# A seventh weight place for the experts, over the residual and the routing scratch

## The chip, the cores and the metric

One core of one Trainium2 chip runs the whole program. The metric is device time in microseconds (us), the median of three runs. The core has TensorE (PE in the profile, its weight loads PEld), VectorE (DVE), ScalarE (ACT), GpSimd (POOL) and SyncE (SP); SyncE does nothing here but issue transfers. Sixteen DMA engines serve the queues of all of them: q1 is SyncE's, q10 is ScalarE's, q0 is GpSimd's.

## The reference

One layer of a hybrid decoder for 512 prompt tokens and 64 sample tokens of width 1024, all in float32. The change touches only its last part: the output projection with the residual, the mixture of experts, and the closing norm.

```python
def finish_layer(x, o_nsa, o_dn, g1, sh2, sc2, g2, lp):
    x = x + g1 * (jnp.concatenate([o_nsa, o_dn], axis=-1) @ lp['w_out'])
    return x + g2 * hier_moe(modulate(x, lp['norm_ffn_g'], sh2, sc2), lp)

def hier_moe(h, lp):
    ...
    for e in range(N_EXPERTS):
        he = jax.nn.silu(x @ lp['w_gate'][e]) * (x @ lp['w_up'][e])
        y = y + gates[:, e:e + 1] * (he @ lp['w_down'][e])
    return y.reshape(B, T, D)

y_prompt = rmsnorm(xp, final_norm_g)
```

The residual `x` after the projection is needed twice: at once, for the normalized rows that are routed, and at the very end, when the experts' sum is added to it. Each token picks one of 4 groups and 2 of its 8 experts. There are 32 experts with three matrices of 1 MiB each (gate, up, down), 1152 routed rows in all (2 for each of 576 tokens).

## The kernel before

The last stage (`stage_moe`, with a helper `slot_parts`) runs in four parts.

1. *Projection and residual*, tile by tile (4 tiles of 128 prompt tokens and one of 64 sample tokens). TensorE multiplies (L2416, L2420), VectorE adds the residual into `m.x2` (L2635), ScalarE squares and takes a root (L2577, L2579), VectorE normalizes into `h2` (L2646, L2647). ScalarE stores the normalized rows to DRAM (L2583, semaphore `h_out`).
2. *Routing.* VectorE and TensorE turn the logits into lists: which rows each expert works on, and which expert stands at which place (`permutation`, semaphore `perm_ok`). The index product is L2462, done with semaphore `ids_ps`. Most of its scratch lies in `m.aux`.
3. *The expert loop.* `ORDER` lists 49 places in a row: 32 base places (one expert each, up to 64 rows) and 17 attached ones, for the rows beyond 64 of an expert. An attached place shares its weights with the base place that `ATTACH` names and stands one base place behind it; if it has no rows, TensorE branches over its products and issues one small product (L2495, L2528) so that the order of the semaphores stays the same. For each place GpSimd gathers 64 rows from DRAM (L2386), TensorE turns them (L2470), multiplies with gate and up (L2483, L2484), turns the hidden rows (L2502) and multiplies with down (L2519, L2520); ScalarE applies silu (L2601) and copies the result out (`take_down`, L2593, L2594), GpSimd scatters it to DRAM (L2392).
4. *The closing.* SyncE loads the two chosen results of each token (L2349) into `rows`, TensorE mixes them with two diagonal matrices `diag` that hold the routing weights (L2561), VectorE scales and adds the residual (L2804 to L2810), then comes the final norm (L2816) and the store.

Weights go through a ring of `RING` places. With 6, they lie in three places of `m.ring`, in `m.late`, in `mod_r` (which holds the modulation rows first) and in `m.h2x` (the normalized rows first). The first `RING` experts are fixed and are loaded before the routing is known; the others are loaded by an index as soon as their place's earlier tenant has been multiplied (`follower`). SyncE issues all of it in the order of its program, each load behind the waits ahead of it. Experts 0 to 2 are asked for at the start, 3 when the projection is done (`y_ps`), 4 when the normalized rows are (`h_ok`), 5 when these have been turned and stored (`hT_ps`, `h_out`).

`m.x2` keeps the residual through the whole loop, and `m.aux` holds the ten diagonal tiles, which ScalarE makes in the middle of the loop (L2608). The closing uses `m.ring` place 2 as scratch (`end`) and reads the results into `m.ring` place 0 and `mod_r`.

Of the kernel before, what the change touches and what calls it, by code (L numbers as in the profile page):

```python
# [14 lines left out]
F32 = mybir.dt.float32  # L15
# [2138 lines left out]
TOPK = 2  # L2154
NOV = TOPK * NTOK // (T + 1)
NT = NE + NOV
RING = 6
KOV = -(-NTOK // T) - 1
DC = DE // P
SLOT = 2 * KD * DE + DC * D  # L2160
NDYN = NE - RING
NPAIR = 12
ATTACH = [RING + 2 * o for o in range(NPAIR)] + [RING + 3 + 4 * k for k in range(NOV - NPAIR)]
ORDER = [x for p in range(NE) for x in [("base", p)] + [("over", o) for o in range(NOV) if ATTACH[o] + 1 == p]]
PLACE = [x if kind == "base" else ATTACH[x] for kind, x in ORDER]
SLOT_OF = [p % RING for p in PLACE]
# [25 lines left out]
def stage_moe(nc, m, sb, sem, t, outs):  # L2192
# [6 lines left out]
    y_ps, x2_ok, sq_ok, rt_ok, h_ok, hT_ps, hT_ok, lg_ps = [sem("r_" + x) for x in ("y_ps", "x2_ok", "sq_ok", "rt_ok", "h_ok", "hT_ps", "hT_ok", "lg_ps")]  # L2199
    chain, pch, exp_in, exp_ok, cnt_ok, cnt_ps, rank_ps = [sem("r_" + x) for x in ("chain", "pch", "exp_in", "exp_ok", "cnt_ok", "cnt_ps", "rank_ps")]  # L2200
    lg_ok, ovf_ok, base_ps, put_ok, ids_ps, ids_ok, te_ok, choice_ok = [sem("r_" + x) for x in ("lg_ok", "ovf_ok", "base_ps", "put_ok", "ids_ps", "ids_ok", "te_ok", "choice_ok")]
    perm_ok = sem("r_perm_ok")
    gu_in, wd_in = [sem(f"gu_in{s}") for s in range(RING)], [sem(f"wd_in{s}") for s in range(RING)]
    r_in, y_out = [sem(f"e_r_in{i}") for i in range(XR)], [sem(f"e_y_out{i}") for i in range(YR)]
    t_ps, t_ok, gu_ps, silu_ok, he_ok, h_ps, heT_ok, dn_ps, yr_ok = [sem("e_" + x) for x in ("t_ps", "t_ok", "gu_ps", "silu_ok", "he_ok", "h_ps", "heT_ok", "dn_ps", "yr_ok")]
# [5 lines left out]
    with ExitStack() as ctx:  # L2211
# [16 lines left out]
        diag = m.aux[:, 0:TOPK * TILES * P].rearrange("p (c i n) -> p c i n", c=TOPK, n=P)  # L2228
        h2 = m.h2x[:, 0:TILES * D].rearrange("p (i n) -> p i n", n=D)
        ht = m.h2x[:, TILES * D:SLOT]  # L2230
        end = m.ring[:, 2]
        mod_f = end[:, 0:2 * D].rearrange("p (v k n) -> p v k n", v=2, k=1)
        fg, junk = end[:, 2 * D:3 * D], end[:, 5 * D:6 * D]
        moved = end[:, 3 * D:5 * D].rearrange("p (s n) -> p s n", s=2)
        rows = [a[:, 0:TILES * D].rearrange("p (i n) -> p i n", n=D) for a in (m.ring[:, 0], modr[:, :])]
        rwe, rwg = h2[:, PT, 0:KD * NE], h2[:, PT, KD * NE:KD * (NE + NG)]

        spare = m.mixT[:, :, :].rearrange("p c n -> p (c n)")
# [22 lines left out]
        same = bo2[0:1, 64:64 + NPAIR]  # L2261
# [13 lines left out]
        def _(sp):  # L2275
# [7 lines left out]

            def load_gate_up(n):
                kind, x = ORDER[n]
                wg, wu, wd = slot_parts(slots[SLOT_OF[n]])
                done = gu_in[SLOT_OF[n]]
                if kind == "base" and x < RING:
                    sp.dma_start(wg, t["expert_w_gate"][0, x].rearrange("(p k) n -> p k n", k=KD)).then_inc(done, 16)
                    sp.dma_start(wu, t["expert_w_up"][0, x].rearrange("(p k) n -> p k n", k=KD)).then_inc(done, 16)  # L2290
                else:
                    e, skip = expert(n)
                    sp.dma_start(wg, t["expert_w_gate"][0, bass.ds(e, 1)].rearrange("o (p k) n -> p (o k) n", k=KD), **skip).then_inc(done, 16)
                    sp.dma_start(wu, t["expert_w_up"][0, bass.ds(e, 1)].rearrange("o (p k) n -> p (o k) n", k=KD), **skip).then_inc(done, 16)

            def load_down(n):
                kind, x = ORDER[n]
                wg, wu, wd = slot_parts(slots[SLOT_OF[n]])
# [21 lines left out]
            load_base(3)  # L2320
            sp.wait_ge(h_ok, TILES)
            load_base(4)
            sp.wait_ge(hT_ps, TILES)
            sp.wait_ge(h_out, 16 * TILES)
            load_base(5)
            sp.wait_ge(perm_ok, 1)

            def follower(n):
# [12 lines left out]
            sp.wait_ge(dn_ps, LAST_USE[NE - RING] + 1)  # L2341
            spread_rows(sp, m, mod_f, 5, 1, f_in)
            sp.dma_start(fg, t["final_norm_g"].partition_broadcast(P)).then_inc(f_in, 16)
            for k in range(YR):
                sp.wait_ge(y_out[k], 16 * ((NT - k + YR - 1) // YR))
            for i in range(TILES):
# [57 lines left out]
        def _(pe):  # L2404
# [68 lines left out]
            def gate_up(n):  # L2473
                kind, x = ORDER[n]
                b = 2 + n % 2
                pe.wait_ge(t_ok, n + 1)
                if n >= 2:
                    pe.wait_ge(he_ok, n - 1)

                def products():  # L2480
                    for q in range(KD):
                        s = dict(start=(q == 0), stop=(q == KD - 1))
                        MM(PS[R, b, 0:DE], xT[:, n % 2, q, :], wg[:, q, :], **s)  # L2483
                        last = MM(PS[Q, b, 0:DE], xT[:, n % 2, q, :], wu[:, q, :], **s)  # L2484
                    return last

                wg, wu, wd = slot_parts(slots[SLOT_OF[n]])
# [17 lines left out]
            def down_products(n):  # L2505
# [4 lines left out]
                    pe.wait_ge(yr_ok, n - 1)  # L2510
                else:
                    pe.wait_ge(put_ok, 1)
                wd = slot_parts(slots[SLOT_OF[n]])[2]
                pe.wait_ge(wd_in[SLOT_OF[n]], 16 * LOADS[n])

                def products():
# [37 lines left out]
            for i in range(TILES):  # L2554
                r, b = ROWS[i], 2 * (i % 4)
                pe.wait_ge(row_in[i], 16 * TOPK)
                if i >= 4:
                    pe.wait_ge(a_ok, i - 3)
                for half in range(2):
                    for c in range(TOPK):  # L2560
                        last = MM(PS[0:r, b + half, :], diag[0:r, c, i, 0:r], rows[c][0:r, i, half * HALF:(half + 1) * HALF], start=(c == 0), stop=(c == 1))  # L2561
                    last.then_inc(f_ps, 1)

        @block.scalar
        def _(act):
# [4 lines left out]
            for i in range(TILES):  # L2570
                r = ROWS[i]
                if i == PT:
                    act.wait_ge(y_ps, TILES)
                    act.wait_ge(rw_ok, 1)
                    nc.scalar.copy(h2[R, PT, HALF:D], PS[Q, 2 * (PT % 2), :]).then_inc(split_ok, 1)
                act.wait_ge(x2_ok, i + 1)
                nc.scalar.activation(h2[0:r, i, :], m.x2[0:r, i, :], ACT.Square, accum_out=ssq[0:r, 0, i:i + 1]).then_inc(sq_ok, 1)  # L2577
                act.wait_ge(sq_ok, i + 1)
                nc.scalar.activation(ssq[0:r, 1, i:i + 1], ssq[0:r, 0, i:i + 1], ACT.Sqrt, scale=1.0 / D, bias=m.eps[0:r, 0:1]).then_inc(rt_ok, 1)  # L2579
            for i in range(TILES):  # L2580
                r = ROWS[i]
                act.wait_ge(h_ok, i + 1)
# [14 lines left out]
            for n in range(NT):  # L2597
# [3 lines left out]
                nc.scalar.activation(sg[Q, n % 2, :], PS[R, 2 + n % 2, 0:DE], ACT.Silu).then_inc(silu_ok, 1)  # L2601
                if n:
                    take_down(n - 1)
                if n == RING:
                    act.wait_ge(choice_ok, 1)
                    for c in range(TOPK):
                        for i in range(TILES):
                            last = nc.scalar.activation(diag[:, c, i, :], m.ident[:, :], ACT.Copy, scale=m.choice[:, c, i:i + 1])  # L2608
                    last.then_inc(diag_ok, 1)
            nc.scalar.activation(wgt[:, 0:1], m.eps[:, 2:3], ACT.Sqrt)  # L2610
            take_down(NT - 1)
            for i in range(TILES):
                r = ROWS[i]
                act.wait_ge(a_ok, i + 1)
# [5 lines left out]
        def _(dve):  # L2620
# [157 lines left out]
            def permutation():  # L2778
# [6 lines left out]
                link(V.tensor_tensor(same, pf[:, 0:2 * NPAIR:2], tef[:, 0:NPAIR], ALU.is_equal))  # L2785
                link(V.tensor_scalar(need, itf[:, :], be[0:1, 1, NE - 1:NE], None, ALU.is_lt))
                link(V.scalar_tensor_tensor(out=need[:, 0:NPAIR], in0=same, scalar=0.5, in1=need[:, 0:NPAIR], op0=ALU.is_lt, op1=ALU.mult))
                V.tensor_copy(pq[:, :], bo2[0:1, 0:NDYN + NOV]).then_inc(perm_ok, 1)

            take_x(0)  # L2790
# [8 lines left out]

            def add(i):  # L2800
                r, v, b = ROWS[i], VAR[i], 2 * (i % 4)
                if i == 0:
                    dve.wait_ge(f_ps, 1)
                    link(V.tensor_tensor(moved[0:r, 0, 0:HALF], PS[0:r, b, :], mod_f[0:r, v, 0, 0:HALF], ALU.mult))  # L2804
# [21 lines left out]
def build(nc, ins, outs):  # L2826
    t = ins
    with ExitStack() as ctx:
# [26 lines left out]
        m.seen = sb("seen", [P, 1])  # L2855
        m.gate_dram = nc.dram_tensor("gate_dram", [NB * TS, 24], F32)
        m.h2_dram = nc.dram_tensor("h2_dram", [NTOK + NT, D], F32)
        m.ys_dram = nc.dram_tensor("ys_dram", [LAST_ROW + 1, D], F32)
        m.choice = sb("choice", [P, TOPK, TILES])
        m.te = sb("te", [1, 2, NOV], I32)  # L2860
# [69 lines left out]
```

## Time and profile before

| | us |
|---|---|
| median of three runs (1067.5 to 1068.67) | 1068.22 |
| the profiled execution, its own time | 1060.37 |
| its span, first to last instruction | 1058.5 |
| TensorE busy in the span | 945.4 |
| VectorE, ScalarE, GpSimd busy | 449.0, 310.4, 268.7 |
| first and last product of the expert loop start | 757.19, 1018.57 |

Durations below come from the profiled execution. The page divides the span in 40 slices of 26.5 us; the expert loop lies in slices 29 to 39. Busy time is the union of an engine's instructions. A transfer has two times: when it is issued (a row of the issuing engine) and when it lands, which the profile tells through semaphores. A row of the chain of waits says who released the next step.

### The profile page before, as it was taken

What the parts mean: (1) busy time and instruction counts of PE and PEld (TensorE: products, weight loads), DVE (VectorE), ACT (ScalarE), POOL (GpSimd) and SP (SyncE); (2) the same over time, 40 slices, a digit from 0 to 9 for tenths busy, and PEclk for the clock granted to TensorE, in tenths of its full rate; (3) what the DMA queues carried; (4) which work ended last, traced back from release to release, by engine and by line L of the source; (5) the groups of instructions that cost most, each with busy time, mean ns of one, the idle gap of its engine ahead of it and who ended that gap; (6) DMA issues with size and microseconds to landing.
All of it is one profiled execution on the core that took longest, in us unless ns stands there. A gap on an engine that the chain in (4) does not pass through costs nothing. (4 is left out here: it accounts for less than half of the span.)

```text
span 1058.5 us, 21135 instructions
## 1 busy us (share of the span) xinstructions
PE 945.4 (89%) x8097; PEld 626.2 (59%) x8097; DVE 449.0 (42%) x933; ACT 310.4 (29%) x712; POOL 268.7 (25%) x397
## 2 busy tenths in 40 slices
PE   6899999998889899998799998996599989888955
PEld 5456777776656768986455664454355555445522
DVE  2330000013767257786478761446522233233317
ACT  4100000002674122333467541111023232333322
POOL 6000000132003048700356432000222333333310
PEclk9999999999999989999599998996599998899988
DMA  9977643433910030000744245908599999999854
GB/s 309 354 282 262 229 160 99 73 95 82 326 42 8 1 49 3 4 4 12 199 111 128 71 170 166 355 24 322 184 372 393 384 394 383 392 375 383 308 179 163
DMA packets 89225, 207.75 MB, mean 196 GB/s; under 512 B 31525, under 2 KB 54749, under 8 KB 75230
## 3 DMA queue, kind: packets, MB, share of 16 engines
q1 hardware_dynamic: 76226, 182.64, 49.4%
q0 software_dynamic: 10144, 20.47, 6.1%
q10 hardware_dynamic: 2756, 3.27, 0.9%
q8 instruction: 69, 1.13, 0.5%
q14 instruction: 30, 0.25, 0.1%
HBM read 254.83 MB, written 29.75 MB: 269 GB/s over the span
## 5 line engine op out<-in xcount | busy, mean ns | idle before, releaser
L2392 POOL DMA_INDIRECT ys_dram<-late,ids x49 | 45.3, 924 | 158.7 <-ACT late L2594 132.3
L592 PE MATMUL PS<-hT,wring 128*128 128x288 f32 x256 | 83.5, 408 | 0.0
L593 PE MATMUL PS<-hT,wring 128*128 128x288 f32 x256 | 83.0, 406 | 0.0
L2776 DVE COPY mixT<-PS 128x128 f32<-128x128 f32 x49 | 14.3, 291 | 155.7 <-PE PS L2502 99.3
L2386 POOL DMA_INDIRECT mixT<-h_dram,ids x49 | 46.9, 956 | 111.4 <-DVE ids L2743 92.4
L2483 PE MATMUL PS<-ring,mixT 128*64 128x256 f32 x304 | 71.4, 389 | 3.7 <-DVE mixT L2762 3.7
L2484 PE MATMUL PS<-ring,mixT 128*64 128x256 f32 x304 | 71.4, 389 | 0.0
L2483 PEld LDWEIGHTS PS<-ring,mixT 128*64 128x64 f32 x304 | 42.4, 141 | 34.1 <-issue 9.8
L2416 PE MATMUL PS<-late,mixT 128*128 128x512 f32 x128 | 58.4, 617 | 1.8 <-PEq L2843 1.8
L592 PEld LDWEIGHTS PS<-hT,wring 128*128 128x128 f32 x256 | 48.2, 190 | 17.2 <-DVE xc L203 2.6
L593 PEld LDWEIGHTS PS<-hT,wring 128*128 128x128 f32 x256 | 48.6, 190 | 13.4
L2593 ACT COPY late<-PS 64x512 f32<-64x512 f32 x49 | 28.3, 578 | 86.3 <-PE PS L2520 69.2
L629 POOL DMA_DIRECT2D late<-in_cache_cmp_k_dram x32 | 17.2, 538 | 132.0 <-issue 132.0
L2416 PEld LDWEIGHTS PS<-late,mixT 128*128 128x128 f32 x128 | 25.2, 199 | 33.0 <-issue 33.0
L2601 ACT ACTIVATE mixT<-PS 64x256 f32<-64x256 f32 x49 | 18.4, 376 | 89.2 <-PE PS L2484 55.9
L2762 DVE COPY mixT<-PS 128x512 f32<-128x512 f32 x49 | 33.8, 691 | 23.3 <-PE PS L2470 22.2
L2484 PEld LDWEIGHTS PS<-ring,mixT 128*64 128x64 f32 x304 | 42.4, 141 | 0.0
L201 DVE COPY xc<-PS 128x288 f32<-128x288 f32 x6 | 2.8, 458 | 92.1 <-PE PS L593 92.1
L2519 PE MATMUL PS<-ring,mixT 128*64 128x512 f32 x76 | 40.2, 655 | 1.0 <-DVE mixT L2776 0.8
L2470 PE MATMUL PS<-ident,mixT 64*128 64x64 f32 x392 | 35.6, 235 | 5.2 <-DMA mixT<-h_dram,ids 5.2
L2520 PE MATMUL PS<-ring,mixT 128*64 128x512 f32 x76 | 40.3, 656 | 0.0
L862 DVE SCALAR_TENSOR_TENSOR acc<-xc,convwT,acc 128x600 f32<-128x600 f32 x36 | 30.1, 843 | 11.6 <-ACT acc L781 10.5
(562 smaller groups left out, 2184.6 us busy)
## 6 DMA issues: line engine op xcount, KB each, us to landing
ring<-in_expert_w_gate_dram SPq DMA_DIRECT2D x27, 1024.0 KB
ring<-in_expert_w_up_dram SPq DMA_DIRECT2D x27, 1024.0 KB
ring<-in_expert_w_down_dram SPq DMA_DIRECT2D x27, 1024.0 KB
late<-in_w_ada_dram SPq DMA_DIRECT2D x8, 2048.0 KB
mod_r<-in_expert_w_gate_dram SPq DMA_DIRECT2D x9, 1024.0 KB
mod_r<-in_expert_w_up_dram SPq DMA_DIRECT2D x9, 1024.0 KB
mod_r<-in_expert_w_down_dram SPq DMA_DIRECT2D x9, 1024.0 KB
late<-in_expert_w_gate_dram SPq DMA_DIRECT2D x7, 1024.0 KB
```

The lines of the kernel that those rows point to most:

```text
L592: MM(PS[:, b, 0:HALF], lhs, hT[:, k, 0:HALF], **s)
L593: last = MM(PS[:, b + 1, 0:HALF], lhs, hT[:, k, HALF:NTOK], **s)
L862: ins = V.scalar_tensor_tensor(out=a, in0=m.xc[:, c, j:j + N], scalar=m.convwT[:, c, j:j + 1], in1=a, op0=ALU.mult, op1=ALU.add)
L2386: pool.indirect_dma_start(xr(n), None, m.h2_dram.ap(), bass.IndirectOffsetOnAxis(ap=ids[:, 0, j:j + 1], axis=0), bounds_check=NTOK + NT - ...
L2392: pool.indirect_dma_start(m.ys_dram.ap(), bass.IndirectOffsetOnAxis(ap=ids[:, 1, j:j + 1], axis=0), yr(n), None, bounds_check=LAST_ROW, oo ...
L2416: last = MM(PS[0:r, b + half, :], m.mixT[:, c, i * P:i * P + r], wo[:, c, half * HALF:(half + 1) * HALF], start=(c == 0), stop=(c == 7))
L2470: last = nc.tensor.transpose(PS[:, n % 2, c * T:(c + 1) * T], xr(n)[:, c * P:(c + 1) * P], m.ident[side(n), side(n)])
L2483: MM(PS[R, b, 0:DE], xT[:, n % 2, q, :], wg[:, q, :], **s)
L2484: last = MM(PS[Q, b, 0:DE], xT[:, n % 2, q, :], wu[:, q, :], **s)
L2519: MM(PS[R, b, :], heT[:, n % 2, c, :], wd[:, c, 0:HALF], **s)
L2520: last = MM(PS[Q, b, :], heT[:, n % 2, c, :], wd[:, c, HALF:], **s)
L2762: V.tensor_copy(xT[:, n % 2], PS[:, n % 2, :].rearrange("p (c n) -> p c n", n=T)).then_inc(t_ok, 1)
```

## The change

`RING` becomes 7. The seventh place lies over the first four tiles of `m.x2` (gate and up) and over `m.aux` (down). Expert 6 becomes a fixed one. ScalarE stores each prompt tile of the residual to DRAM (`x2_dram`) right after its root, and SyncE loads the four tiles back late in the loop; VectorE waits for each before it adds (`x_back`). The diagonal tiles move behind the last place of the loop and into `m.ring` places 0 and 1; the closing's scratch moves to `mod_r`. All attached places move back by one. `NPAIR` is only renamed.

```diff
-RING = 6
+RING = 7
...
+        diag = [m.ring[:, c, TILES * D:TILES * D + TILES * P].rearrange("p (i n) -> p i n", n=P) for c in range(TOPK)]
+        of_x2 = m.x2[:, :, :].rearrange("p i n -> p (i n)")
+
+        def parts(s):
+            if s < len(slots):
+                return slot_parts(slots[s])
+            return (of_x2[:, 0:KD * DE].rearrange("p (k n) -> p k n", n=DE), of_x2[:, KD * DE:2 * KD * DE].rearrange("p (k n) -> p k n", n=DE),
+                    m.aux[:, 0:DC * D].rearrange("p (c n) -> p c n", n=D))
...
-        end = m.ring[:, 2]
+        end = modr[:, :]
...
-        rows = [a[:, 0:TILES * D].rearrange("p (i n) -> p i n", n=D) for a in (m.ring[:, 0], modr[:, :])]
+        rows = [a[:, 0:TILES * D].rearrange("p (i n) -> p i n", n=D) for a in (m.ring[:, 0], m.ring[:, 1])]
...
             sp.wait_ge(h_ok, TILES)
             load_base(4)
+            sp.wait_ge(x_out, 16 * PT)
+            load_gate_up(6)
             sp.wait_ge(hT_ps, TILES)
             sp.wait_ge(h_out, 16 * TILES)
             load_base(5)
+            sp.wait_ge(ids_ps, 1)
+            load_down(6)
             sp.wait_ge(perm_ok, 1)
...
             sp.dma_start(fg, t["final_norm_g"].partition_broadcast(P)).then_inc(f_in, 16)
+            sp.wait_ge(dn_ps, LAST_USE[NE - RING + 2] + 1)
+            for i in range(PT):
+                sp.dma_start(m.x2[:, i, :], m.x2_dram.ap()[i * P:(i + 1) * P, :]).then_inc(x_back[i], 16)
...
                 nc.scalar.activation(ssq[0:r, 1, i:i + 1], ssq[0:r, 0, i:i + 1], ACT.Sqrt, scale=1.0 / D, bias=m.eps[0:r, 0:1]).then_inc(rt_ok, 1)
+                if i < PT:
+                    act.dma_start(m.x2_dram.ap()[i * P:(i + 1) * P, :], m.x2[:, i, :]).then_inc(x_out, 16)
...
-                if n == RING:
-                    act.wait_ge(choice_ok, 1)
-                    for c in range(TOPK):
-                        for i in range(TILES):
-                            last = nc.scalar.activation(diag[:, c, i, :], m.ident[:, :], ACT.Copy, scale=m.choice[:, c, i:i + 1])
-                    last.then_inc(diag_ok, 1)
             nc.scalar.activation(wgt[:, 0:1], m.eps[:, 2:3], ACT.Sqrt)
             take_down(NT - 1)
+            act.wait_ge(choice_ok, 1)
+            for i in range(TILES):
+                for c in range(TOPK):
+                    last = nc.scalar.activation(diag[c][:, i, :], m.ident[:, :], ACT.Copy, scale=m.choice[:, c, i:i + 1])
+            last.then_inc(diag_ok, 1)
...
             def add(i):
                 r, v, b = ROWS[i], VAR[i], 2 * (i % 4)
+                if i < PT:
+                    dve.wait_ge(x_back[i], 16)
```

How the instructions stand. First SyncE before the routing's result, from expert 4 (in `mod_r`) to the first read of the permutation (`pq`), before the change:

```order
L2289 DMA mod_r<-in_expert_w_gate_dram 128x2048
L2290 DMA mod_r<-in_expert_w_up_dram 128x2048
L2301 DMA mod_r<-in_expert_w_down_dram 128x2048
L2289 DMA h2x<-in_expert_w_gate_dram 128x2048
L2290 DMA h2x<-in_expert_w_up_dram 128x2048
L2301 DMA h2x<-in_expert_w_down_dram 128x2048
L2279 TENSOR_LOAD pq
```

And the same place after the change (`x` is `m.x2`, `h2x` holds expert 5):

```order
L2296 DMA mod_r<-in_expert_w_gate_dram 128x2048
L2297 DMA mod_r<-in_expert_w_up_dram 128x2048
L2308 DMA mod_r<-in_expert_w_down_dram 128x2048
L2296 DMA x<-in_expert_w_gate_dram 128x2048
L2297 DMA x<-in_expert_w_up_dram 128x2048
L2296 DMA h2x<-in_expert_w_gate_dram 128x2048
L2297 DMA h2x<-in_expert_w_up_dram 128x2048
L2308 DMA h2x<-in_expert_w_down_dram 128x2048
L2308 DMA aux<-in_expert_w_down_dram 128x2048
L2286 TENSOR_LOAD pq
```

Two transfers of 1 MiB have come in ahead of expert 5 and one behind it.

ScalarE at the end of the loop, from the load of the root's table to the closing's first square, before the change:

```order
L2610 ACT_TABLE_LOAD
L2610 ACTIVATE wgt<-eps 128x1
L2593 COPY late<-PS 64x512
L2594 COPY late<-PS 64x512
L2615 ACTIVATE ring,ssq_r<-x2 128x1024
```

And after it:

```order
L2620 ACT_TABLE_LOAD
L2620 ACTIVATE wgt<-eps 128x1
L2609 COPY late<-PS 64x512
L2610 COPY late<-PS 64x512
L2625 ACTIVATE ring<-ident,choice 128x128 x10
L2630 ACTIVATE mod_r,ssq_r<-x2 128x1024
```

The ten diagonal tiles now stand between the last copy of the loop and the closing. SyncE's last instructions after the change, from the modulation rows to the stores:

```order
L104 DMA mod_r<-mod_dram 128x1024
L106 DMA mod_r<-mod_dram 8x1024 x8
L2354 DMA mod_r<-in_final_norm_g_dram 128x1024
L2357 DMA x<-x_dram 128x1024 x4
L2363 DMA ring<-ys_dram 128x1024 x8
L2363 DMA ring<-ys_dram 64x1024 x2
L2367 DMA out_dram<-x 128x1024 x4
```

The line L2357 is new: the residual comes back between the norm's gain and the chosen results.

## Rows read from the trace of the kernel before

**Rows 1.** The page: busy tenths of the DMA engines in 40 equal slices.
```profile
DMA  9977643433910030000744245908599999999854
```

**Rows 2.** Stretches of the stage: us, busy time of each engine (instructions), clock, DMA share, GB/s.
```profile
core 0: us, PE busy (x) PEld busy (x) DVE busy (x) ACT busy (x) POOL busy (x), PEclk, DMA share, GB/s
690.00:718.00 28.00, 28.00 (x118) 14.33 (x116) 14.22 (x14) 2.89 (x6) 0.00 (x0) 1.00 0.02 7
742.00:752.00 10.00, 2.86 (x20) 2.42 (x20) 6.50 (x21) 0.00 (x0) 0.00 (x0) 0.50 0.79 315
752.00:754.00 2.00, 0.00 (x0) 0.00 (x0) 1.77 (x8) 0.00 (x0) 1.40 (x2) 0.50 0.00 0
764.00:980.00 216.00, 196.49 (x1590) 113.75 (x1592) 65.29 (x124) 65.80 (x133) 74.04 (x79) 0.95 1.01 381
1000.00:1005.00 5.00, 4.99 (x40) 2.54 (x40) 3.19 (x6) 1.91 (x4) 0.33 (x1) 1.00 0.42 166
```

**Rows 3.** Waits of TensorE in the expert loop: us in total, times, longest.
```profile
PE PS L2528 <- DVE mixT L2776: 9.7, 10, 1.7
PE PS L2483 <- DVE mixT L2762: 5.2, 8, 1.0
```

**Rows 4.** The chain of waits at the start of the loop: start us, us, what.
```profile
752.29 2.96 DMA mixT<-h_dram,ids
755.29 1.12 PE PS L2470 x8
757.19 0.69 PE PS L2483
```

**Rows 5.** Timeline of ScalarE, SyncE and TensorE: start us, us, engine line op.
```profile
712.40 0.29 ACT L2579 ACTIVATE ssq_r<-ssq_r,eps 128x1 f32<-128x1 f32 x1
...
726.85 0.50 SPq L2301 DMA_DIRECT2D mod_r<-in_expert_w_down_dram  x1
...
743.15 0.43 SPq L2301 DMA_DIRECT2D h2x<-in_expert_w_down_dram  x1
...
980.79 0.34 SPq L2293 DMA_DIRECT2D ring<-in_expert_w_gate_dram  x1
...
1004.25 0.34 SPq L104 DMA_DIRECT2D ring<-mod_dram  x1
...
1010.32 0.43 PE L2483 MATMUL PS<-ring,mixT 128*64 128x256 f32 x1 [0.36 <-DVE mixT L2762]
```

**Rows 6.** Queues from 728 to 742 us: packets, MB, share of the engines.
```profile
q1 hardware_dynamic: 481, 3.42, 59.1%
q10 hardware_dynamic: 603, 2.14, 37.4%
```

**Rows 7.** The five stores of the normalized rows (L2583).
```profile
DMA to landing us min/median/max: 8.6/15.1/17.8
```

**Rows 8.** The seventh gather; queues at 764.6 to 768, 768 to 770, 770 to 773.8.
```profile
764.68 0.94 POOL L2386 DMA_INDIRECT mixT<-h_dram,ids  x1 [4.73 <-PE PS L2470]
...
q1 hardware_dynamic: 107, 0.88, 71.3%
...
q0 software_dynamic: 26, 0.11, 15.4%
...
q0 software_dynamic: 54, 0.16, 16.0%
```

**Rows 9.** The ten diagonal tiles (L2608), and the chain of waits behind the loop.
```profile
L2608 ACT ACTIVATE aux<-ident,choice x10: 387/388/400, 802.4 to 805.0; 128x128 f32<-128x128 f32 x10
...
1019.91 0.59 ACT late L2594
1021.29 2.54 DMA ys_dram<-late,ids
...
1024.23 4.26 DMA mod_r<-ys_dram
1028.63 8.67 PE PS L2561 x16
```

More of the change, by code:

```diff
@@ L2161 @@
 NDYN = NE - RING
-NPAIR = 12
-ATTACH = [RING + 2 * o for o in range(NPAIR)] + [RING + 3 + 4 * k for k in range(NOV - NPAIR)]
+NMATCH = 12
+ATTACH = [RING + 2 * o for o in range(NMATCH)] + [RING + 3 + 4 * k for k in range(NOV - NMATCH)]
 ORDER = [x for p in range(NE) for x in [("base", p)] + [("over", o) for o in range(NOV) if ATTACH[o] + 1 == p]]
@@ L2201, in stage_moe @@
     lg_ok, ovf_ok, base_ps, put_ok, ids_ps, ids_ok, te_ok, choice_ok = [sem("r_" + x) for x in ("lg_ok", "ovf_ok", "base_ps", "put_ok", "ids_ps", "ids_ok", "te_ok", "choice_ok")]
-    perm_ok = sem("r_perm_ok")
+    perm_ok, x_out, x_back = sem("r_perm_ok"), sem("r_x_out"), [sem(f"f_x_back{i}") for i in range(PT)]
     gu_in, wd_in = [sem(f"gu_in{s}") for s in range(RING)], [sem(f"wd_in{s}") for s in range(RING)]
@@ L2227, in stage_moe @@
         bo2 = tmp_late[0:NE, 15 * D // 8:2 * D]
-        diag = m.aux[:, 0:TOPK * TILES * P].rearrange("p (c i n) -> p c i n", c=TOPK, n=P)
+        diag = [m.ring[:, c, TILES * D:TILES * D + TILES * P].rearrange("p (i n) -> p i n", n=P) for c in range(TOPK)]
[5 more added lines that the diff above has]
+                    m.aux[:, 0:DC * D].rearrange("p (c n) -> p c n", n=D))
         h2 = m.h2x[:, 0:TILES * D].rearrange("p (i n) -> p i n", n=D)
         ht = m.h2x[:, TILES * D:SLOT]
-        end = m.ring[:, 2]
+        end = modr[:, :]
         mod_f = end[:, 0:2 * D].rearrange("p (v k n) -> p v k n", v=2, k=1)
@@ L2260, in stage_moe @@
         pf, need = bo2[0:1, 0:NDYN], bo2[0:1, NDYN:NDYN + NOV]
-        same = bo2[0:1, 64:64 + NPAIR]
+        same = bo2[0:1, 64:64 + NMATCH]
         a4 = tb("a4", [P, TILES, NG])
@@ L2285, in load_gate_up @@
                 kind, x = ORDER[n]
-                wg, wu, wd = slot_parts(slots[SLOT_OF[n]])
+                wg, wu, wd = parts(SLOT_OF[n])
                 done = gu_in[SLOT_OF[n]]
@@ L2297, in load_down @@
                 kind, x = ORDER[n]
-                wg, wu, wd = slot_parts(slots[SLOT_OF[n]])
+                wg, wu, wd = parts(SLOT_OF[n])
                 done = wd_in[SLOT_OF[n]]
@@ L2485, in products @@
                     return last
-                wg, wu, wd = slot_parts(slots[SLOT_OF[n]])
+                wg, wu, wd = parts(SLOT_OF[n])
                 pe.wait_ge(gu_in[SLOT_OF[n]], 32 * LOADS[n])
@@ L2512, in down_products @@
                     pe.wait_ge(put_ok, 1)
-                wd = slot_parts(slots[SLOT_OF[n]])[2]
+                wd = parts(SLOT_OF[n])[2]
                 pe.wait_ge(wd_in[SLOT_OF[n]], 16 * LOADS[n])
@@ L2560, in _ @@
                     for c in range(TOPK):
-                        last = MM(PS[0:r, b + half, :], diag[0:r, c, i, 0:r], rows[c][0:r, i, half * HALF:(half + 1) * HALF], start=(c == 0), stop=(c == 1))
+                        last = MM(PS[0:r, b + half, :], diag[c][0:r, i, 0:r], rows[c][0:r, i, half * HALF:(half + 1) * HALF], start=(c == 0), stop=(c == 1))
                     last.then_inc(f_ps, 1)
@@ L2784, in permutation @@
                 link(V.tensor_scalar(pf, pf, -1.0, float(NE), ALU.mult, ALU.add))
-                link(V.tensor_tensor(same, pf[:, 0:2 * NPAIR:2], tef[:, 0:NPAIR], ALU.is_equal))
+                link(V.tensor_tensor(same, pf[:, 0:2 * NMATCH:2], tef[:, 0:NMATCH], ALU.is_equal))
                 link(V.tensor_scalar(need, itf[:, :], be[0:1, 1, NE - 1:NE], None, ALU.is_lt))
-                link(V.scalar_tensor_tensor(out=need[:, 0:NPAIR], in0=same, scalar=0.5, in1=need[:, 0:NPAIR], op0=ALU.is_lt, op1=ALU.mult))
+                link(V.scalar_tensor_tensor(out=need[:, 0:NMATCH], in0=same, scalar=0.5, in1=need[:, 0:NMATCH], op0=ALU.is_lt, op1=ALU.mult))
                 V.tensor_copy(pq[:, :], bo2[0:1, 0:NDYN + NOV]).then_inc(perm_ok, 1)
@@ L2857, in build @@
         m.h2_dram = nc.dram_tensor("h2_dram", [NTOK + NT, D], F32)
+        m.x2_dram = nc.dram_tensor("x2_dram", [SEQ, D], F32)
         m.ys_dram = nc.dram_tensor("ys_dram", [LAST_ROW + 1, D], F32)
```

## The prediction

> **What bounds the kernel now.** I read the page first. The DMA engines are full in the first quarter, nearly idle in the middle, and at nine tenths from slice 28 to slice 37, which is where the experts are worked through [rows 1]. That invites the reading "the expert loop waits for weights, so one more place for weights must help". The table by stretches sharpens it: from 764 to 980 us the DMA share is 1.01 at 381 GB/s, and TensorE is busy 196.5 of the same 216 us [rows 2]. Both are near their limit, so busy shares cannot say which of them sets the pace. The list of TensorE's waits in the loop can: its two largest entries are waits for a VectorE copy (9.7 and 5.2 us in total) [rows 3], and no weight tile stands anywhere in it. The larger is at L2528, the small product that an attached expert without rows still issues. So TensorE never meets a late weight; it loses time to the short dependent steps of the empty places and to its clock: a mean of 0.95 over 216 us [rows 2] is some 21.6 us at the lower level (0.05 x 216 x 2), which costs about 10.8 us.
>
> How far is the weight stream from being felt? The gate half of the last expert is asked for at 980.79 and first multiplied at 1010.32, after 0.36 us of waiting for a copy [rows 5]; the DMA share has fallen to 0.42 in 1000 to 1005 [rows 2]. So I take it that the last weights were there about 5 us before their use. That is the slack, and it is small: 5 of 243 us.
>
> At the front of the loop the chain of waits holds exactly one transfer. The indices are ready, the first gather is issued at 752.29, and 2.96 us later TensorE starts to turn its rows [rows 4]. From 752 to 754 the DMA engines move nothing, share 0.00 [rows 2]: the gather finds empty queues.
>
> **The change part by part.**
>
> *The seventh place.* It lets expert 6 (3.15 MB in gate, up and down) be loaded before the loop, so the loop streams 25 experts in place of 26. At 381 GB/s that is 3.15 / 0.381 = 8.3 us less streaming. But the list of waits shows nothing that ends when weights land, so by this profile it buys 0: it only raises the slack of 5 us.
>
> *Where its load lies.* Expert 6's gate and up are issued behind expert 4's, whose last part is issued at 726.85 [rows 5], and its down behind expert 5's, once the index product is done. In the kernel before, expert 5 is asked for at 743.15 (its last part) [rows 5] and those 3.15 MB move in 742 to 752 (0.315 x 10) [rows 2]; then the queue is dry. Now the same queue, served in order, has 2.1 MB ahead of expert 5 and 1.05 MB behind it: 3.15 MB more. The rate from 728 to 742 was (3.42 + 2.14) / 14 = 0.397 MB per us [rows 6], so the extra takes 7.9 us, of which about 2 us fill the gap between expert 5's issue and its first byte (8 us of transfer at that rate in a 10 us stretch). The queue is dry at about 752 + 7.9 - 2 = 758, not at 752. The first gather is still issued at 752.3, since nothing in the index chain changes, and now meets a full queue.
>
> What does a gather take beside full queues? The first one took 2.96 us. The seventh is issued at 764.68, just behind 2.1 MB of weights. Until 768 only the weight queue moves data (0.88 MB, no row of q0); the gather's queue moves 0.11 MB in 768 to 770 and 0.16 MB in 770 to 773.8 [rows 8]. It was not let through at its turn; it came in 5 to 9 us. The five 512 KB stores of the normalized rows, beside experts 3 and 4, took 8.6 to 17.8 us each [rows 7]. So I take it that the first gather lands when the weights ahead of it are through: at about 758.2 in place of 755.25, **+3.0 us**, straight on the path. Bounds: at the low end the gather gets a fair share. Then its at most 0.26 MB move at half of 0.397 MB per us in place of all of it: 1.3 us against 0.7, **+0.7**. At the high end it takes what the seventh took, up to 9.1 us: **+6.1**.
>
> The Trainium skill, "DMA: Bandwidth & Descriptors", section "Queues, rings and completion order", says that each DMA engine goes round between the queues that have work, a packet at a time; by it the gather would be let in at once and the term would be the low end. The trace agrees for the stores beside the weights, which had 37.4 of 96.5 points of the share [rows 6], and does not for the seventh gather.
>
> *The stores of the residual.* Four stores of 512 KB, issued by ScalarE after each tile's root, the last behind the one at 712.40 [rows 5]. ScalarE is busy 2.89 of 28 us there, and the queues have a share of 0.02 from 690 to 718 [rows 2]. 2.1 MB at 0.397 is 5.3 us in a hole of 28. The one wait on them stands on SyncE behind expert 4's issue at 726.85, 14 us after the last store. Behind it are queued experts 5 and 6 only. Price 0; without the hole it would be 5.3 us.
>
> *Normalized rows.* They share with expert 4 up to 742, as before; expert 6 queues behind expert 4. SyncE waits for them before it issues expert 5, so they had landed by 743, and POOL's wait for them has 9 us to spare before 752. Price 0.
>
> *The diagonal tiles.* Ten activations of 388 ns [rows 9], 3.9 us, leave the loop, where ScalarE is busy 65.8 of 216 us [rows 2] and nobody waits for them: 0. They now stand behind the last take_down, from 1020.5 to 1024.4. TensorE needs them with the first rows, which it gets at 1028.6, behind the last scatter (2.54 us) and the loads (4.26 us) [rows 9]. Cover 4.2 us: 0. Should the rows come sooner, at most 3.9.
>
> *The residual's return.* Four loads of 512 KB on SyncE, behind the modulation rows and ahead of its wait for the last scatter. Before, the modulation rows were issued at 1004.25 [rows 5], behind the last attached place; in the new order that place stands one expert later, so the return is issued about 1010. It needs 5.3 us and is wanted by VectorE only with TensorE's closing products, the first of which starts at 1028.6 [rows 9]. Price 0; it also ends before the last scatter at 1021.
>
> *The attached products.* All 17 move by one place, with the same numbers of full and of empty ones, if no expert with more than 64 rows is among the first seven (rival D). Price 0. Each shift of the pattern can move the clock's low stretches; with 10.8 us lost to them in all I allow 2 us either way.
>
> Sum: +3.0 + 0 + 0 + 0 + 0 = **+3 us**. The profiled execution has a span of 1058.5 us and a time of 1060.37; it would become 1063.4. The three timed runs have a median of 1068.22, 7.85 above the profiled execution, so I forecast 1068.22 + 3 = **1071.2 us**.
>
> **The rivals.**
>
> *A, the stream is felt in the timed runs (faster).* For: the timed runs take 7.85 us longer than the profiled one, and the slack is only about 5 us. If those 7.85 us lie in slower transfers, the last experts wait for weights, and 8.3 us less streaming pay. Against: a constant piece outside the span would look the same. The weight stream also starts 3 us later, so the gain is 8.3 - 3 = 5.3 us: 1062.9.
>
> *B, the gather is let in (no change).* The front costs 0.7 us and the rest nothing: 1068.9. For it the shares of rows 6, against it rows 8. A small gain inside the loop would give the same picture.
>
> *C, the front costs more (slower).* The gather takes as long as the seventh did, +6.1: 1074.3. For: rows 8. Against: the queue in front of it is finite and dry at 758, while in the loop it is refilled all the time.
>
> *D, the extra place does not help because an overflowing expert is now a fixed one.* Then one attached expert must be loaded again: 8.3 us more streaming, which eats the advantage; with the slack unused it ends as the forecast does. Its chance is inside the forecast's.
>
> **How the numbers follow.** Forecast 0.40, A 0.27, B 0.23, C 0.10. A measurement here can tell about 0.2%, 2.1 us, from no change. The forecast's own spread is 2 us for the clock, so a sixth of it falls within 2.1 us; A falls nearly all below; C all above. That gives faster 0.27, same 0.28 (B and some of the forecast), slower 0.45. The range leaves out a little of A at its lower and of C at its upper end: 1062.0 to 1075.0. The forecast's own range is 1068.9 (the low bound of the gather) to 1074.3 (the high bound).
>
> **What would show it.** Right: in the chain of waits at the start of the loop the one transfer of the first gather has grown from 2.96 to about 6 us, the DMA share in 752 to 754 is near 1 and not 0.00, the first product starts near 760, the length from there to the last product is 262 us within 2, and the closing takes what it took. Wrong: a first product at 757 to 758 (B); a loop shorter than 262 us by more than 3 with TensorE's waits at L2528 and L2495 unchanged, which would mean that contention and not lateness of weights was the price of the full queues; or a wait for the residual or the diagonals in the closing.

## The result, and the profile after

| us | before | after |
|---|---|---|
| median (20 runs each, in turns on the same chips) | 1064.38 (1059.09 to 1068.67) | 1068.82 (1062.36 to 1076.09) |
| ratio, 95% interval | | 1.0045 [1.0027, 1.0063] |
| the profiled execution, its own time | 1060.37 | 1069.76 |
| its span | 1058.5 | 1067.9 |

The change makes the kernel slower, by about 4.4 us. Every ratio here and below leaves out the executions that are over 1.5% longer than the fastest of the same kernel, so it can differ a little from the quotient of two medians. The two profiled executions differ by 9.4 us, and most of that is not the change's: the indices are ready 6.3 us later already (757.46 for 751.17 us), and the code ahead of this stage is the same. So the stretches are compared from there on, not the clock times.

The page of after (busy tenths of the DMA engines in 40 slices; ScalarE's queue, 3.27 MB before) and the same stretches of the windows view:

```profile
DMA  9976642432910030000744244928799999999674
...
q10 hardware_dynamic: 3332, 5.36, 1.4%
```
```profile
core 0: us, PE busy (x) PEld busy (x) DVE busy (x) ACT busy (x) POOL busy (x), PEclk, DMA share, GB/s
752.00:754.00 2.00, 0.46 (x4) 0.46 (x5) 1.45 (x3) 0.00 (x0) 0.00 (x0) 0.50 0.98 369
...
758.00:764.00 6.00, 0.00 (x0) 0.00 (x0) 2.21 (x10) 0.00 (x0) 4.20 (x5) 0.50 1.01 382
764.00:980.00 216.00, 198.94 (x1613) 115.54 (x1613) 67.51 (x128) 61.51 (x119) 75.33 (x81) 0.95 0.98 364
1000.00:1005.00 5.00, 5.00 (x27) 2.11 (x26) 1.57 (x3) 1.21 (x3) 0.93 (x1) 0.66 0.60 228
```

The hole ahead of the loop [rows 2] is closed: the share is 0.98 from 752 to 754, where it was 0.00, and 1.01 from 758 to 764, which is where that moment lies in this later execution. The queues in 760 to 762 and in 762 to 764, while the first gather (issued at 758.59) is under way:

```profile
q1 hardware_dynamic: 118, 0.84, 100.3%
...
q0 software_dynamic: 169, 0.32, 69.2%
q1 hardware_dynamic: 47, 0.25, 31.8%
```

Until 762 only the weights move (q1); the gather's queue (q0) gets its first bytes after that. The chain of waits at the start of the loop, against [rows 4] (start us, us, what):

```profile
758.59 6.22 DMA mixT<-h_dram,ids
...
764.86 1.13 PE PS L2484 x8
...
766.75 0.69 PE PS L2497
```

The gather takes 6.22 us in place of 2.96: **+3.3 us**. TensorE's waits in the loop, against [rows 3] and one more row of before, for the other small product:

```profile
PE PS L2495 <- DVE mixT L2762: 5.2, 9, 1.1
```

The small products (now L2542, L2509) wait less, but now three products wait for weights, 6.9 us in all.

```profile
PE PS L2509 <- DVE mixT L2777: 4.8, 9, 0.6
PE PS L2509 <- DMA mod_r<-in_expert_w_up_dram: 3.2, 1, 3.2
PE PS L2542 <- DVE mixT L2791: 2.9, 10, 0.6
PE PS L2497 <- DMA h2x<-in_expert_w_up_dram: 2.7, 1, 2.7
...
PE PS L2509 <- DMA ring<-in_expert_w_up_dram: 1.0, 1, 1.0
```

The chain behind the loop, against [rows 9], and SyncE and ScalarE beside it in the timeline:

```profile
1027.22 5.56 DMA ys_dram<-late,ids
...
1033.16 4.25 DMA ring<-ys_dram
...
1037.54 2.90 PE PS L2575 x3
```
```profile
1016.70 0.34 SPq L104 DMA_DIRECT2D mod_r<-mod_dram  x1
1017.08 2.71 SPq L106 DMA_DIRECT2D mod_r<-mod_dram  x8
1019.83 0.37 SPq L2354 DMA_DIRECT2D mod_r<-in_final_norm_g_dram  x1
1020.24 2.13 SPq L2357 DMA_DIRECT2D x<-x_dram  x4
1032.80 5.39 SPq L2363 DMA_DIRECT2D ring<-ys_dram  x10
...
1026.33 3.03 ACT L2625 ACTIVATE ring<-ident,choice 128x128 f32<-128x128 f32 x10
```

The last scatter takes 5.56 us in place of 2.54: **+3.0 us**. The residual is asked for at 1020.24 to 1022.37, behind the modulation rows, and from 1024 to 1030 the engines are full (share 1.01, then 0.94). From 1027 to 1032.8 SyncE's queue still moves 1.20 MB, 0.98 MB of it before 1030. The residual's four loads take 8.2 to 10.9 us each from issue to landing. The diagonal tiles end at 1029.4, 8 us ahead of their first use.

From the indices to the end it is thus 310.4 us in place of 307.3, but the loop between the two new waits (first gate product to last down product) is 257.9 us in place of 261.4. That the loop is shorter is the one thing the two traces leave open, and the first question for a run.

### The profile page after: what moved, and what is told of

The parts are those of the page before. It is cut to its first block and busy times, and to the rows that moved or that the text cites. A ratio compares the mean times of both kernels' runs of the same rounds, so it can differ in the third digit from the quotient of the medians.

```text
span 1067.9 us, 21135 instructions
## 1 busy us (share of the span) xinstructions
PE 952.5 (89%) x8097; PEld 630.7 (59%) x8097; DVE 449.0 (42%) x933; ACT 310.3 (29%) x712; POOL 268.5 (25%) x397
## 5 line engine op out<-in xcount | busy, mean ns | idle before, releaser
L2497 PE MATMUL PS<-ring,mixT 128*64 128x256 f32 x272 | 64.4, 392 | 2.4 <-DVE mixT L2777 2.4
L2498 PE MATMUL PS<-ring,mixT 128*64 128x256 f32 x272 | 64.4, 392 | 0.0
L2497 PEld LDWEIGHTS PS<-ring,mixT 128*64 128x64 f32 x272 | 38.4, 143 | 30.3 <-issue 10.9
L2777 DVE COPY mixT<-PS 128x512 f32<-128x512 f32 x49 | 33.9, 692 | 16.1 <-PE PS L2484 14.2
L2498 PEld LDWEIGHTS PS<-ring,mixT 128*64 128x64 f32 x272 | 38.4, 143 | 0.0
L1001 PE MATMUL PS<-xT,kvt 128*128 128x289 f32 x128 | 33.9, 425 | 2.2 <-issue 2.2
L2533 PE MATMUL PS<-ring,mixT 128*64 128x512 f32 x68 | 34.5, 631 | 0.1
```

Source lines behind the costliest of these rows:

```text
L1001: last = MM(PS[:, 2 + u % 2, 0:HCOL + 1], W1[s][:, l, c * P:(c + 1) * P], xT[:, v, l % OCT, l // OCT:l // OCT + HCOL + 1], start=(l == 0), ...
L2533: MM(PS[R, b, :], heT[:, n % 2, c, :], wd[:, c, 0:HALF], **s)
L2777: V.tensor_copy(xT[:, n % 2], PS[:, n % 2, :].rearrange("p (c n) -> p c n", n=T)).then_inc(t_ok, 1)
```

## The experiments

Twelve runs, in order. The front and end columns are lengths in the chain of waits; "copies" is VectorE's idle time before its 49 copies of the turned rows (L2762 in before) until TensorE releases them; "weights" is TensorE's waits for weights in the loop.

| profile | chip | first gather | loop | last scatter | copies | weights |
|---|---|---|---|---|---|---|
| before, as shown first | ? | 2.96 | 261.4 | 2.54 | 22.2 | 0 |
| after, as shown first | ? | 6.22 | 257.9 | 5.56 | 14.2 | 6.9 |
| before_again | 8 | 2.87 | 256.4 | 2.55 | 10.5 | 2.8 |
| e1_down_late | 8 | 3.60 | 256.6 | 4.99 | 11.0 | 1.7 |
| e2_return_early | 8 | 5.90 | 257.3 | 2.85 | 13.7 | 5.1 |
| e3_both | 8 | 3.08 | 256.8 | 2.86 | 10.6 | 2.1 |
| after_again | 10 | 7.45 | 262.9 | 4.60 | 25.7 | 0 |
| e3_both_again | 10 | 3.3 | 264.8 | 2.87 | 21.7 | 0 |
| e4_no_early_start | 10 | 3.2 | 265.0 | 2.86 | 22.2 | 0 |
| e5_return_alone | 10 | 2.99 | 261.0 | 2.54 | 21.7 | 0 |
| e6_return_behind_rows | 10 | 3.01 | 262.9 | 2.54 | 22.5 | 0 |
| e7_one_expert_less | 10 | 2.86 | 261.5 | 2.54 | 21.6 | 0 |
| e8_four_experts_less | 10 | 2.90 | 263.6 | 2.53 | 19.9 | 0 |
| e4_again | 10 | 2.85 | 261.9 | 2.86 | 23.4 | 1.4 |

(Two of the gathers, 3.3 and 3.2, are read from the gather's issue to the first turn.) The chip of the first two profiles is not recorded.

**before_again**: the kernel before, unchanged.

> The kernel before once more, for a second trace. In its first trace the stage began at 647.0 us and every turn of gathered rows from the 4th to the 42nd was seen by VectorE 0.6 to 1.3 us after its recorded end; in the trace after the change the stage began at 653.4 and no turn was seen late. If both are properties of an execution and not of the code (theory), this trace shows either pair freely: a stage start anywhere in 647 to 654, and late turns absent or present whatever the start. If the late turns belong to the code of before (rival), they are here again, in 35 or more of 49 places, and the loop takes 261 us within 1.5.

1064.26 us, span 1062.4. The group of the copies in the first profile of before (us idle before it, times), and in this one:

```profile
its engine sat idle before it (us, times) until:
  PE PS L2470: 22.2, 35
```
```profile
its engine sat idle before it (us, times) until:
  PE PS L2470: 10.5, 27
```

The turn and the copy of the fourth place, first profile and this one (timeline: start us, us; in brackets the idle time before):

```profile
774.51 0.66 PE L2470 MATMUL PS<-ident,mixT 64*128 64x64 f32 x8
...
775.79 0.69 DVE L2762 COPY mixT<-PS 128x512 f32<-128x512 f32 x1 [0.79 <-PE PS L2470]
```
```profile
782.56 0.66 PE L2470 MATMUL PS<-ident,mixT 64*128 64x64 f32 x8
...
783.26 0.69 DVE L2762 COPY mixT<-PS 128x512 f32<-128x512 f32 x1 [0.21 <-PE PS L2470]
```

The turn ends at 775.17 and at 783.22; the copy begins 0.62 us later in one and 0.04 in the other. In the first profile 21 of the 49 copies are late like this, by 0.6 to 1.3 us (and one by 0.2), not every one from the 4th to the 42nd as the expectation has it; in the second none. The stage began at 655.0 us, just outside the 647 to 654 expected. Without that lateness the loop takes 256.4 us, not 261.4, and TensorE catches up with the weights:

```profile
PE PS L2483 <- DMA mod_r<-in_expert_w_up_dram: 2.2, 1, 2.2
PE PS L2483 <- DMA ring<-in_expert_w_up_dram: 0.6, 1, 0.6
```

So the 3.5 us by which the loop of after was shorter are put down to the execution and not to the change: like beside like, and across jobs, 256.4 (here) stands beside 257.9 and 261.4 beside 262.9 in after_again.

**e1_down_late, e2_return_early, e3_both**: the changed kernel with one or both of the collisions taken away.

```diff
 # e1, e3
-            sp.wait_ge(ids_ps, 1)
-            load_down(6)
             sp.wait_ge(perm_ok, 1)
+            load_down(6)
 # e2, e3: the four loads in SyncE's loop, where the place is free, and no longer behind the modulation rows
+                if n == LAST_USE[NE - RING + 2] + 1:
+                    sp.wait_ge(dn_ps, n)
+                    for i in range(PT): ... x2 <- x2_dram
```

> The changed kernel, but expert 6's down part (1 MiB) is issued behind the wait for the permutation and not behind the index product. Theory: the first gather waits for whatever weights are queued ahead of it; in the changed kernel only this 1 MiB was still moving when it was issued. Then its time falls from 6.22 back to about 3.0 us and the kernel gains 3.2 us on the changed one (ratio to before about 1.001). Rival (the gather gets a fair share, and it was slow for some other reason such as the descriptors of two queues): it stays at 5 us or more and the ratio stays at 1.0045.

> The changed kernel, but the residual's four loads are issued inside the loop, as soon as place 27 has been multiplied, and not behind the modulation rows. Theory: in the changed kernel they (2.1 MB behind 1.3 MB) still filled the queues at 1027 when the last scatter was issued, and it took 5.58 us from issue to the first row load, against 2.56 before. With the early return it is 2.6 to 3.2 us again, and the kernel gains 2.5 to 3 us on the changed one. Rival (the scatter is late because ScalarE now writes ten diagonal tiles beside it): it stays at 5.5 us.

> Both edits: the down part of expert 6 behind the permutation, the residual's return inside the loop. Theory (the two waits for queues are separate and add): 6 us less than the changed kernel, so a ratio to before of 0.998 to 1.000, or lower if the loop is really shorter with the seventh place. Rival (the loop is bound by the weight stream, so an earlier start only makes TensorE wait more for weights): 3 us or less of gain on the changed kernel, with TensorE's waits for weights grown by the rest.

Measured in one job: 1.0034 [1.0009, 1.0058], 1.0030 [1.0008, 1.0053] and 0.9969 [0.9946, 0.9991]; medians 1066.28, 1064.35 and 1059.94 beside 1064.25. Chains at the front and at the end of e1:

```profile
758.34 3.60 DMA mixT<-h_dram,ids
...
1023.13 4.99 DMA ys_dram<-late,ids
```

of e2:

```profile
753.96 5.90 DMA mixT<-h_dram,ids
...
1021.72 2.85 DMA ys_dram<-late,ids
```

and of e3:

```profile
761.88 3.08 DMA mixT<-h_dram,ids
...
1026.31 2.86 DMA ys_dram<-late,ids
```

Each edit takes away its own wait and leaves the other. The last 1 MiB alone (down of expert 6) held the first gather by 2.6 us (after against e1) and 2.8 (e2 against e3), and the return alone the last scatter by 2.7 us (after against e2) and 2.1 (e1 against e3). The times are less clean. Beside the changed kernel's 1.0045, which is from another job, the ratios of e1 and e2 are 1.2 and 1.6 us better, where some 3 us each were expected, and that of e3 is 8 us better, where 6 were; an interval reaches over 2 us to either side, so the ratios do not show the two gains one by one. e3 is the one version that was faster than the kernel before.

**after_again, e3_both_again, e4_no_early_start, e5_return_alone**, one job on another chip. e4 is e3 with all of expert 6 behind the permutation:

```diff
             sp.wait_ge(x_out, 16 * PT)
-            load_gate_up(6)
...
             sp.wait_ge(perm_ok, 1)
+            load_gate_up(6)
             load_down(6)
```

e5 is the kernel before with the four stores, the four waits and, behind the modulation rows,

```diff
+            sp.wait_ge(x_out, 16 * PT)
+            sp.wait_ge(gu_ps, NT)
+            for i in range(PT): ... x2 <- x2_dram
```

> The changed kernel as it is, so that the variants stand beside it on one chip. Both theories: about 4.4 us over the kernel before (ratio 1.003 to 1.006). Theory (two collisions, at the front and at the end): in its profile the first gather takes 5.5 to 6.5 us and the last scatter is followed by the first load of results after 5 to 6 us. If these two differ from the first profile of this kernel (6.2 and 5.6), they are properties of an execution and not of the order of the transfers.

> Both repairs once more (down of expert 6 asked for when the permutation is ready, the residual's return issued inside the loop), in the same job as the changed kernel. Theory (each collision costs about 3 us and the seventh place itself gains some 3 us): 6 to 8 us less than the changed kernel, 2 to 4 us less than the kernel before (ratio 0.996 to 0.998). Rival (the place buys nothing and the first result was luck): equal to the kernel before within 0.15%.

> As the version with both repairs, but gate and up of expert 6 too are asked for only when the permutation is ready, so that nothing of the seventh place is loaded while the DMA engines would be idle before the loop; the depth of seven places stays. Theory (what the place gains is that 3.15 MB are streamed before the loop): the gain of 3.3 us over the kernel before shrinks to about 1 us or less, since 2.1 MB of it (5.5 us of streaming) are in the loop again: ratio 0.999 to 1.001. Rival (it is the depth that gains, a later weight is covered by a longer queue): as with both repairs, ratio 0.996 to 0.998. Gather in either case 2.9 to 3.6 us.

> The kernel before, six places, with the residual's round trip alone: the four stores behind the roots, and the four loads issued when the last gate and up products are done (about 1014 to 1016 us), some 4 us ahead of the last down product, as in the changed kernel. Theory (the return is still moving when the last scatter is issued): the time from the last scatter's issue to the first load of results grows from 2.56 to 5 to 6 us and the median by about 3 us, ratio 1.002 to 1.004; the first gather stays at 2.9 us. Rival (the late scatter in the changed kernel comes from something else of the change, the diagonals or the ring): 2.6 us and ratio 0.999 to 1.001.

Ratios to before: after 1.0056 [1.0024, 1.0088], e3 1.0015 [0.9984, 1.0047], e4 1.0043 [1.0005, 1.008], e5 1.0 [0.9966, 1.0034]; medians of all their runs 1073.92, 1070.92, 1070.17 and 1069.66 beside 1069.55. e4 is above both of its expectations. The changed kernel repeats, with a gather of 7.45 and a scatter of 4.60, both a little outside what was expected. **e3's gain does not repeat here**, and my expectation for it was wrong. What differs is in the table: all profiles of this chip have the late copies, the loop is 5 us longer for the changed kernel and 8 for e3, and no product waits for weights. e5 came out against my expectation too: the return, issued at 1020.45, was nearly through when the last scatter was issued at 1027.66, as the windows show, and the scatter took 2.54.

```profile
1026.00:1028.00 2.00, 0.00 (x0) 0.00 (x0) 0.00 (x0) 0.85 (x2) 0.34 (x1) 0.97 0.87 342
1028.00:1030.00 2.00, 0.00 (x0) 0.00 (x0) 0.00 (x0) 0.00 (x0) 0.55 (x1) 0.50 0.32 84
```

So the return as such costs nothing that this run can show; where it costs, it is still moving in bulk at the last scatter.

**e6_return_behind_rows**: e5 with the modulation rows held back too.

```diff
             sp.wait_ge(dn_ps, LAST_USE[NE - RING] + 1)
+            sp.wait_ge(gu_ps, NT - 1)
             spread_rows(sp, m, mod_f, 5, 1, f_in)
```

> The kernel before with the residual's round trip alone, as in the run before, but the modulation rows (0.5 MB and eight times 32 KB) and the norm's gain (0.5 MB) are asked for only when the last but one gate and up products are done, so that the return stands behind them in one full queue, as in the changed kernel. Theory (what hurts the last scatter is that 3.4 MB are asked for within its last 11 us): from the last scatter's issue to the first load of results 4.5 to 6 us instead of 2.56, and DMA share near 1 in the 2 us after the scatter's issue; the median 2 to 3.5 us over the kernel before, ratio 1.001 to 1.004. Rival (the diagonals or the places of the results in the ring cause it): 2.6 us, ratio 1.0 within 0.15%.

1.0032 [0.9992, 1.0072]; the scatter took 2.54: not what I expected. The rows were issued 12.4 us ahead of the scatter (1010.59 and 1023.03) where the changed kernel has 10.5 (1016.70 and 1027.22), and the queue was nearly clear again:

```profile
1020.00:1022.00 2.00, 0.90 (x6) 0.02 (x2) 0.00 (x0) 1.97 (x4) 0.89 (x1) 1.00 0.96 377
1022.00:1024.00 2.00, 0.00 (x0) 0.00 (x0) 0.00 (x0) 0.23 (x1) 0.90 (x1) 1.00 0.68 264
```

I missed the collision by 2 us, so the kernel before was never made slow by the return. That the return causes it in the changed kernel rests on the two pairs that differ in its place alone (after and e2, e1 and e3), and the other profiles fit: 5.56, 4.60 and (e1) 4.99 us with it late, 2.85 to 2.87 in all five profiles with it early.

**e7_one_expert_less, e8_four_experts_less** (weights left out) and **e4_again**, in the job of e6:

```diff
+                elif kind == "base" and x == RING:      # e8: x in range(RING, RING + 4)
+                    sp.dma_start(wg[:, 0:1, :], ...); sp.dma_start(wu[:, 0:1, :], ...)   # down: wd[:, 0:1, :]
```

> The kernel before, six places, but of expert 6, the first that is streamed in the loop, only an eighth of gate and up and half of down is loaded (the rest of its weights is left out): 2.36 MB less in the loop, the seventh place's gain without its price at the front and at the end. Theory (what the stream costs depends on the execution's pace, and this is a property of the chip: where the turned rows are handed over 0.7 us late in half of the places, the loop is some 5 us longer and no product waits for weights): with late handovers in its own profile no wait for weights and a ratio of 1.0 within 0.2%; without them the waits for weights vanish from its profile and the ratio is 0.996 to 0.999. Rival (the place gains everywhere): 0.996 to 0.999 in either case.

> As the one before, but with experts 6 to 9 cut the same way (the rest of their weights is left out): 9.4 MB, some 25 us of the stream, less, so that weights are early everywhere. Theory: with late handovers still a ratio of 1.0 within 0.3%, and the loop from the first to the last product as long as in the kernel before (261 to 265 us): transfers do not set the pace. Without late handovers the ratio is 0.995 to 0.998 and no more, since only the 3 to 5 us of waits for weights can go. Rival (contention with the stream slows the small transfers and the handovers): the loop becomes shorter by 5 us or more and the late handovers go away where the stream is thinner.

> The version with both repairs and no early start of expert 6's load once more. Theory: with late handovers as in its first run (equal to the version with both repairs, 1 us over the kernel before at the same clock); without them the waits for weights are back (2 to 4 us in its profile), ratio 0.998 to 1.001. Rival (the depth of seven places gains by itself): no waits for weights, ratio 0.996 to 0.998.

Ratios 1.0031 [0.9996, 1.0065], 1.0026 [1.0, 1.0053] and 1.0015 [0.9979, 1.0051]. e7 lies outside the 0.2% expected, with an interval that holds 1.0. e4 has late copies again and, against the expectation, one wait for weights beside them (1.4 us). With 9.4 MB less the engines have air in the first 80 us of the loop (e8, windows):

```profile
764.00:804.00 40.00, 39.21 (x330) 22.43 (x332) 10.92 (x20) 11.74 (x24) 10.37 (x12) 1.00 0.69 230
804.00:844.00 40.00, 39.83 (x336) 23.73 (x334) 11.17 (x21) 12.80 (x29) 13.48 (x15) 1.00 0.86 324
```

and the loop is still 263.6 us, with the late copies still there (19.9 us). So on this chip the stream sets no pace, a thinner stream does not take the lateness of the copies away (9 of the 18 late ones begin before 844), and a seventh place has nothing to give that these runs could see.

**The clock as a second reading.** Within a job the time follows the granted clock of the execution: a common slope fitted to the runs of a job is 6.6 to 9.0 us for 0.01. Read at the same clock, the distance to before is +0.1 (e1), +0.3 (e2), -2.7 (e3) on chip 8, and +3.6 (after), +1.2 (e3), +1.5 and +1.1 (e4), -0.3 (e5), +0.7 (e6), -0.3 (e7), -0.7 us (e8) on chip 10, each within about 1 us by the scatter of 1.4 to 1.6 us that is left. So e1 and e2 stand 2.8 and 3.0 us above e3, near the size of the wait that each keeps (2.1 and 2.8 us). This was fitted afterwards, and the change may itself move the clock, so it only supports the ratios: e3 gains on one chip and not on the other, and e8 gains next to nothing.

## Why the prediction was right, and where not

1071.2 us was forecast, +3.0 on the median shown; measured are +4.4 on the median of 20, and 1068.82 us. The time came near for a reason that is only in part mine.

*The front: right, and well sized.* +3.0 forecast by "lands when the weights ahead of it are through", +3.3 measured, 7.45 us at the worst (bounds +0.7 to +6.1). Rival B is out: the gather was not let in at once. With the 1 MiB ahead of it moved away it took 3.60 us in place of 6.22, so what counts is what stands in the other queue. The Trainium skill, "DMA: Bandwidth & Descriptors", section "Queues, rings and completion order", says that each DMA engine takes turns between the queues that have work, a packet at a time. By the prediction's reading of that rule the term would have been +0.7; the trace does not agree, since from 760 to 762 the gather's queue moved nothing while the weights moved 0.84 MB.

*The residual's return: wrong.* By the prediction it "is issued about 1010" and "ends before the last scatter at 1021", price 0. It was issued at 1020.24, 7 us ahead of the scatter, behind rows that were issued only at 1016.70 (1004.25 before), and was still moving when the scatter was issued: +3.0 us. Two things were left out. The place that SyncE waits for moved by 6.2 us (1016.70 - 1004.25, less the 6.3 us of the later execution), near the 5.8 I took for it (1010 less 1004.25); but issuing the rows and the gain takes SyncE another 3.5 us (1016.70 to 1020.24), so the return is issued at 1014 on the clock of before and not at 1010. And "It needs 5.3 us" lets it start at its issue, with 1.3 MB of rows and gain ahead of it in the same queue; it took 8.2 to 10.9 us here, and 3.3 to 7.0 us in e5, where the rows were issued 10 us ahead of it.

Even this does not close it: 3.4 MB at the 0.397 MB per us of [rows 6], from 1010.4 on, would be through at 1019. While the rows moved and the return had just been issued, the engines moved less than that:

```profile
1020.00:1022.00 2.00, 1.53 (x14) 0.77 (x10) 0.40 (x2) 0.38 (x1) 0.71 (x1) 1.00 0.76 252
1022.00:1024.00 2.00, 1.35 (x8) 0.73 (x10) 0.79 (x2) 1.48 (x3) 0.00 (x0) 1.00 0.62 135
```

Why they did is open.

The mixing products that want the residual were never late; the scatter that shares the engines with it was.

*The loop: half right.* "TensorE never meets a late weight" was true of the profile I had, and of seven of the eight on chip 10; e7 and e8 show that there the place is worth 0. It was not true of the five profiles without late copies, where weights are waited for by 1.7 to 6.9 us. I took a property of one execution for one of the kernel. Of the signs that I had named, the first product near 760 came (766.75, less the 6.3 us), but the loop of 262 us within 2 did not (257.9), nor did a closing that takes what it took. Rival A named the other side (a stream that is felt), but put it on slower transfers; it is felt where the loop is *faster*. There the version with both repairs gained some 3 us (e3, -3.3 by its ratio). That this is the place's own gain is my reading and not shown: the loop of e3's profile is no shorter.

*The sum.* Front +3.3 and end +3.0 are 6.3 us in the traces; the medians say 4.4. The rest may be the place's gain on chips like chip 8, but on chip 10 after and e3 differ by 3.0 us in the medians and by 5.9 in front and end of their profiles, so the two are not closed to better than 2 to 3 us. That the forecast of +3.0 came near +4.4 is thus in part luck: a term of 3 us was priced at nothing, and something of 2 us that is not shown went the other way. The chances do not add up either: a sixth of the forecast's 0.40 beside B's 0.23 is 0.30 for the same time and 0.43 for slower, not 0.28 and 0.45.

*Priced at nothing, and nothing:* the stores (e5 at 1.0), the diagonal tiles (8 us of cover left), the attached products (not seen apart). Rival C's +6.1 is the size of front and end together, but not its mechanism; rival D was not seen apart.

*Open:* why the copies of turned rows come late, mostly by 0.6 to 1.4 us, on one chip and not on the other (only between the fourth and the 45th place, in about half of them), and whether it is the chip at all, since chip 8 stands for one job and chip 10 for two; and in which waits e3's gain lies, since its one profile, at one of its slowest runs, shows a loop of 256.8 us beside 256.4. Not tried: the changed kernel in one job with e3, and e4, on a chip without late copies.

## What to carry to other kernels

Let a prefetch into idle engines be through before the next small transfer on the critical path is issued, at the front as at the end: give it the issue point that lets it finish, and count everything ahead of it in its queue. Here two loads that nobody was waiting for made a wait of 3 us each, and moving their issue took both waits away in every profile; what that gives in time was seen on one chip (e3, -3.3 us to before) and only in part on the other. Before a "nothing waits for this" is put in a sum, look at a second execution, better on another chip: with a slack of 2% of the loop, as here, what TensorE waits for changed from one to the other.

## What the runs showed of the hardware

Chip 8 (one job) ran loops of 256 to 258 us, chip 10 (two jobs) of 261 to 265 us; e3 ran on both, with 256.8 and 264.8. In every profile of the slower one 18 to 24 of the 49 copies behind a turn start late, mostly by 0.6 to 1.4 us. The start of the stage, in untouched code, lay between 647 and 658.5 us. The first gather took 2.9 to 3.6 us without the late 1 MiB ahead of it and 5.9 to 7.5 us with it; the last scatter 2.5 to 2.9 us against 4.6 to 5.6.
